# RMSNorms in blocks of 344 tokens inside the phase that uses them, in a float32 hybrid decoder step

## The reference

```python
def rmsnorm(x, g):
    return x * lax.rsqrt(jnp.mean(x * x, axis=-1, keepdims=True) + EPS) * g
def swiglu(h, w_in, w_out):
    gu = h @ w_in
    return (jax.nn.silu(gu[..., :2816]) * gu[..., 2816:]) @ w_out
for i in range(2):
    hn = rmsnorm(x, norm_mix_g[i])
    x = x + (gated_deltanet(hn, ...) if i == 0 else s5_mixer(hn, ...))
    x = x + swiglu(rmsnorm(x, norm_ffn_g[i]), w_ffn_in[i], w_ffn_out[i])
y = rmsnorm(x, final_norm_g)
```

## Time and profile before

| | us |
|---|---|
| median of 3 executions | 3890.07 |
| the profiled execution | 3887.29 |
| its span, first to last instruction | 3885.5 |
| PE busy / DVE / ACT / POOL | 3545.1 / 2123.1 / 845.5 / 836.9 |
| mean granted TensorE clock | 0.959 |

### The profile page before, as it was taken

One profiled execution on the slowest core, in us unless ns is written; L12 is line 12 of the kernel. 1 busy time (PEld: TensorE's weight loads), 2 busy tenths in 40 slices (PEclk: granted clock), 3 DMA queues, 4 the chain that ended last, 5 costly groups with the idle time before them and its releaser, 6 DMA issues.

```text
span 3885.5 us, 56613 instructions
## 1 busy us (share of the span) xinstructions
PE 3545.1 (91%) x23849; PEld 3439.2 (89%) x23849; DVE 2123.1 (55%) x4331; ACT 845.5 (22%) x1691; POOL 836.9 (22%) x773
## 2 busy tenths in 40 slices
PE   4999999999999999997889999997679699999997
PEld 3989999998989898996879999996569699999997
DVE  3576757566666767575477577554632333333424
ACT  2333232423333332323100110111210210000001
POOL 1202020201111020201223232322323133323331
PEclk7999999999999999999989999999779899999998
DMA  2101010101001010100112222223831011111111
GB/s 78 34 23 36 28 41 17 41 23 40 29 30 40 23 36 28 35 17 29 33 40 75 71 70 77 71 77 110 231 90 49 22 44 49 44 50 49 45 49 55
DMA packets 91965, 197.29 MB, mean 51 GB/s; under 512 B 23232, under 2 KB 51008, under 8 KB 90560
## 3 DMA queue, kind: packets, MB, share of 16 engines
q1 hardware_dynamic: 65344, 152.42, 12.1%
q10 hardware_dynamic: 26368, 41.25, 3.2%
HBM read 152.69 MB, written 40.94 MB: 50 GB/s over the span
## 4 chain that ended last, share of the span: by engine, by line
PE 78%; DVE 17%; issue 2%; ACT 2%; DMA 1%; SPq 1%; POOL 0%; ACTq 0%; DVEq 0%; POOLq 0%
PE ps L210 25%; PE ps L464 14%; PE ps L1162 11%; PE ps L634 4%; PE ps L548 4%; PE ps L630 4%; PE ps L620 3%; PE ps L240 2%; PE ps L488 1%; DVE dwork L1095 1%; PE ps L523 1%; PE ps L536 1%; DVE hlo L269 1%; DVE S L987 1%; PE ps L476 1%
## 5 line engine op out<-in xcount | busy, mean ns | idle before, releaser
L210 PE MATMUL ps<-hhi,whi 128*128 128x344 f32 x2520 | 811.5, 322 | 87.2 <-DVE hlo L269 72.2
L210 PE MATMUL ps<-hhi,wlo 128*128 128x344 f32 x2520 | 808.8, 321 | 0.0
L210 PE MATMUL ps<-hlo,whi 128*128 128x344 f32 x2520 | 807.9, 321 | 0.0
L1843 POOL TENSOR_TENSOR wtick<-wtick 128x1 f32<-128x1 f32 x213 | 43.0, 202 | 2846.8 <-PE ps L210 977.6
L210 PEld LDWEIGHTS ps<-hhi,whi 128*128 128x128 f32 x2520 | 477.4, 189 | 90.5 <-issue 66.2
L1846 POOL TENSOR_TENSOR wlo<-wraw,whi 128x1024 fp32r<-128x1024 f32 x213 | 527.5, 2477 | 17.1
L210 PEld LDWEIGHTS ps<-hhi,wlo 128*128 128x128 f32 x2520 | 476.8, 189 | 0.0
L210 PEld LDWEIGHTS ps<-hlo,whi 128*128 128x128 f32 x2520 | 476.5, 189 | 0.0
L1215 DVE TENSOR_TENSOR ab<-ps,sg 128x344 f32<-128x344 f32 x132 | 68.2, 516 | 639.5 <-PE ps L210 628.1
L464 PE MATMUL ps<-hhi,whi 128*128 128x344 f32 x1152 | 386.2, 335 | 4.4 <-DVE dwork L847 1.9
L1162 PE MATMUL ps<-ahi,whi 128*128 128x344 f32 x1056 | 342.7, 325 | 32.3 <-DVE ab L1215 29.9
(11 more groups left out here) (328 smaller groups left out, 6092.2 us busy)
## 6 DMA issues: line engine op xcount, KB each, us to landing
wraw<-in_w SPq DMA_DIRECT2D x213, 512.0 KB, 3.3
tab<-keep_tab SPq DMA_DIRECT2D x8, 1088.0 KB, 6.4
S<-in_sin ACTq DMA_DIRECT2D x16, 512.0 KB, 3.5
out_sout<-S ACTq DMA_DIRECT2D x16, 512.0 KB, 2.6
keep_u<-hs SPq DMA_DIRECT2D x8, 580.0 KB, 3.0
uu<-keep_u SPq DMA_DIRECT2D x8, 580.0 KB, 7.9
keep_tab<-cp ACTq DMA_DIRECT2D x8, 576.0 KB, 6.1
keep_y<-yg SPq DMA_DIRECT2D x64, 68.5 KB, 2.3
```

The source lines that it names most:

```text
L210: ins = nc.tensor.matmul(out, w, r[:, kt, blk(n)], start=k == 0, stop=k == 3 * KT - 1)
```

## The change

**By blocks.** The prolog's, the two FFN norms and the last one go by blocks of 344 tokens. Squares and `nh` now lie in a ring of six places of 344 columns in the same memory (`RING`). DVE makes part of the squares: in block 0 the odd tiles, in block 1 tiles 0 to 3; in the last norm the odd tiles of block 2. `nh`, `hhi` and `hlo` of block 0 can be made when block 0's sums are there.

**In one phase.** n1, n3 and fin are no phases any more. ffn0 and ffn1 begin with the norm: PE makes the sums of blocks 0 and 1, then, when block 0 is ready, the gate and the up unit of f = 0, j = 0 for block 0 alone (`project_pair`); then the sums of block 2, the pair for block 1, the pair for block 2. In the prolog PE makes all 24 sums and then projects block by block. ffn1's last output units go block by block too (`piece`), with the last norm's sums of a block behind the next block's pieces.

**Issue.** The operations are issued by `go`, with waits for single steps. x is loaded in three transfers, one a block, and y stored in four (block 0, block 1, two halves of block 2). The ACT table is loaded ahead of the wait for x in the prolog, and right behind the last `ahi` copy in ffn1.

```diff
+        def project_pair(p, units, banks, names, ready):
+            at = [wait_weights(p, u) for u in units]
+            for n in range(NC3):
+                ready(n)
+                for u, s, bank, name in zip(units, at, banks, names):
+                    out = ps[:, bank(n), 0:NB]
...
+                    p.go(ins, f"{name}{n}")
+                    plan[("PE", f"unit{u}")] = p.n
+        RING = 6
+        def square_by(n, kt, last=False):
+            if last:
+                return "DVE" if n == 2 and kt % 2 else "ACT"
+            return "DVE" if (n == 0 and kt % 2) or (n == 1 and kt < 4) else "ACT"
+        def sums(p, n, bank, last=False):
+            w = "f" if last else ""
+            b = bank("ACT", w + f"ln{n}")
+            for kt in range(KT):
+                p.after(square_by(n, kt, last), w + f"sq{n}.{kt}")
+                p.go(nc.tensor.matmul(ps[:, b, 0:NB], ones[:, :], ring(nsq, KT * n + kt), ...), w + f"ss{n}.{kt}")
+        def square(e, n, kt, ready=None, last=False):
+            k = KT * n + kt
+            if k >= RING:
+                e.after("PE", w + f"ss{(k - RING) // KT}.{(k - RING) % KT}")
...
+        def norm_blocks_act(a, ready=None):
+            nc.scalar.preload_act_table_set(LOGEXP)
+            mine = [(n, kt) for n in range(NC3) for kt in range(KT) if square_by(n, kt) == "ACT"]
+            ahead = [s for s in mine if KT * s[0] + s[1] < KT + RING]
+            rest = mine[len(ahead):]
+            for n, kt in ahead:
+                square(a, n, kt, ready)
+            for n in range(NC3):
+                root(a, n)
+                for kt in range(KT):
+                    a.after("DVE", f"h{n}.{kt}")
+                    a.go(nc.scalar.activation(hhi[:, kt, blk(n)], ring(nh, KT * n + kt), AF.Copy), f"hi{n}.{kt}")
+                    if rest and (n == 0 or kt < 2):
+                        square(a, *rest.pop(0), ready)
+        def norm_blocks_dve(v, gi, ready=None):
...
+            for k in range(NC3 * KT + 2):
+                n, kt = divmod(k, KT)
+                if n < NC3:
+                    if k >= RING:
+                        v.after("DVE", f"lo{(k - RING) // KT}.{(k - RING) % KT}")
+                    v.after("ACT", f"rms{n}")
+                    v.go(V.scalar_tensor_tensor(ring(nh, k), x[:, kt, blk(n)], gains[:, gi, kt:kt + 1], nr[:, blk(n)], ALU.mult, ALU.mult), f"h{n}.{kt}")
+                if k >= 2:
+                    n, kt = divmod(k - 2, KT)
+                    v.after("ACT", f"hi{n}.{kt}")
+                    v.go(V.tensor_tensor(hlo[:, kt, blk(n)], ring(nh, k - 2), hhi[:, kt, blk(n)].bitcast(F32), ALU.subtract), f"lo{n}.{kt}")
...
         def ffn_pe(ph):
+                sums(p, 0, take)
+                sums(p, 1, take)
+                def block_ready(n):
+                    if n == 1:
+                        sums(p, 2, take)
+                    normed(p, n)
...
+                        if ph == "ffn1" and f == NF:
+                            for n in range(NC3):
+                                for m in range(KT):
+                                    piece(m, n)
+                                if n:
+                                    sums(p, n - 1, take, True)
+                            sums(p, NC3 - 1, take, True)
...
         def ffn_act(ph):
+                norm_blocks_act(a)
...
+                if ph == "ffn1":
+                    nc.scalar.preload_act_table_set(LOGEXP)
+                    for n, kt in mine[:KT + RING]:
+                        square(a, n, kt, added, True)
+                    root(a, 0, True)
+                    for n, kt in mine[KT + RING:]:
+                        square(a, n, kt, added, True)
+                    root(a, 1, True)
+                    store_y(a, 0, 0, KT)
+                    root(a, 2, True)
+                    store_y(a, 1, 0, KT)
+                    store_y(a, 2, 0, KT // 2)
+                    store_y(a, 2, KT // 2, KT)
...
         def ffn_dve(ph):
+                norm_blocks_dve(v, 1 if ph == "ffn0" else 3)
...
+                    for kt in range(1, KT, 2):
+                        square(v, NC3 - 1, kt, added, True)
+                    for n in range(NC3):
+                        v.after("ACT", f"frms{n}")
+                        for kt in range(KT):
+                            v.go(V.scalar_tensor_tensor(x[:, kt, blk(n)], ...), f"y{n}.{kt}")
...
-            sp.dma_start(x[:, :, :], dr["x"]).then_inc(in_x, 16)
+            for n in range(NC3):
+                sp.dma_start(x[:, :, blk(n)], dr["x"][:, :, blk(n)]).then_inc(in_x[n], 16)
```

More of the change, by code:

```diff
@@ L79, in build @@
         const_ready = sem("const_ready")
-        in_x = sem("in_x")
+        in_x = [sem(f"in_x{n}") for n in range(NC3)]
         in_par = sem("in_par")
@@ new lines, in square @@
+        def square(e, n, kt, ready=None, last=False):
+            w = "f" if last else ""
+            k = KT * n + kt
+            if k >= RING:
+                e.after("PE", w + f"ss{(k - RING) // KT}.{(k - RING) % KT}")
+            if ready is not None:
+                ready(n, kt)
+            if e.who == "ACT":
+                e.go(nc.scalar.activation(ring(nsq, k), x[:, kt, blk(n)], AF.Square), w + f"sq{n}.{kt}")
+            else:
+                e.go(nc.vector.tensor_tensor(ring(nsq, k), x[:, kt, blk(n)], x[:, kt, blk(n)], ALU.mult), w + f"sq{n}.{kt}")
@@ L271, in build, with normed @@
+        def normed(p, n):
+            p.after("DVE", f"lo{n}.{KT - 1}")
         eps_t = sb("eps_t", [P, 4])
@@ L1166, in ffn_pe, with piece @@
-            return body
+                        def piece(m, n):
+                            s = wait_weights(p, unit(ph, e, 4 + m // 4))
+                            out = ps[:, take("DVE", f"x{e}.{m}.{n}"), 0:NB]
+                            q = 0
+                            for kt in range(2):
+                                c = kt * 512 + m % 4 * P
+                                for w, r in ((whi, ahi), (whi, alo), (wlo, ahi)):
+                                    ins = nc.tensor.matmul(out, w[:, s, c:c + P], r[:, e % 2, kt, blk(n)], start=q == 0, stop=q == 5)
+                                    q += 1
+                            p.go(ins, f"out{e}.{m}.{n}")
+                            if n == NC3 - 1:
+                                plan[("PE", f"unit{unit(ph, e, 4 + m // 4)}")] = p.n
```

118 lines of the change are left out of this document (57 added, 61 removed).

## The result

The changed kernel took 3840.6 us (median of four runs, 3840.5 to 3841.4) where the kernel before took 3888.8; the ratio is 0.9879, 95% interval 0.9862 to 0.9896. Forecast were 3831 and the range 3818 to 3849. The unaltered changed kernel, run again in a later session, took 3845.5, ratio 0.9901 (0.9885 to 0.9918). So 38 to 48 us are saved of the 56.5 that the prediction added up (before took 3883.1 beside the later runs).

What follows compares the result with a forecast made beforehand. Four serial stages holding 165 us were taken as what the change touches: prolog 23.0, FFN norms 12.2 and 10.4, tail 10.9 saved, 56.5 in sum. From 3887.3 that gives 3830.8, stated as 3831; own range 3824 to 3840, whole range 3818 to 3849.

Steps and rivals of the forecast that it cites:

- the four serial stages: Prolog, two FFN norms and tail: three engines work in turn, none full; they hold 165 us, gains forecast at 56.5.
- hidden by that: FFN norms, POOL's 3.6 us split for the next weight slot: covered by the slot being freed 3.8 earlier, so no cost.
- Rival A: Small operations don't overlap on their engine once each has its own wait: 3847 us; chance 0.16.
- stall: FFN norms: ACT, and DVE with it, stands 11.7 us at block 2's square until that block's first sum frees a ring place.
- the price of the second clock fall: First FFN norm, PE's gap of 4.4 us: if the clock falls there too, 2.7 us, ending at 55.3 instead of 52.7.
- the charge of 0.7 for the squares beside a split: First FFN norm: POOL splits until 1819.2 and may slow DVE's new squares; 0.7 us off the gain, bounds 0 to 2.3.
- Rival B: The clock holds in the gaps of 4.4 us and nothing collides on the port: 3822 us; chance 0.14.
- Rival D: The clock stays low in the four stages as PE works in bursts: slower than before, 3923 us; chance 0.02.
- I charge 2 of 6.8: Prolog: POOL's splits of weight units 0 and 1 beside h and lo cost 2 us of 6.8, bounds 0 and 6.8.
- Rival C: Prolog: x in short rows lands slowly, so the prolog's whole gain is gone: 3855 us; chance 0.05.
- a start after 11: Prolog: the first sum, forecast at 10.6 us; starting after 11 was named as a sign that the prediction is wrong.
- The last store then takes what it takes now: Tail: from the last product y to the end of the span 3.1 us, as in the kernel before.

## Why the prediction was right, and where it was off

*The bound.* Right: the four serial stages held the time and gave 52.8 of the 56.5 us forecast. Not all that moved outside them is scatter: 1.9 us in FFN 0 and 0.5 in FFN 1 came with the new norms. 0.5 of each is a term that the prediction put at nothing, the split "hidden by that" behind the pair: PE waited 0.2 for it, and the unit took 11.80 for 11.32.

*Prices of small operations.* Right: product and subtraction came at 0.92 a tile, the y products at 0.49. Rival A (no overlap) is out.

*First and second FFN norm.* The order of events was right, and most times to 0.3: stall 11.80 for 11.7, pauses 7.0 and 4.2 for 7.3 and 4.4, block 0 ready at 18.6 for 18.4, block 1 at 37.7 for 37.5. Off was the price of the second clock fall: 2.7 taken for each, and with the clock held the run shows 2.5 for the first and 1.55 for the second. Too high too was the charge of 0.7 for the squares beside a split: they did collide (one square took 2.67 for 0.50), but the first root was done 8.3 after the table load for 8.1. So the ends came at 54.7 for 55.3, and 55.9 or 57.5 for 58.2. Rival B had the clock hold in the short pause; the windows show it at 0.50. Rival D had it stay low; over the two norms it is 0.88 and 0.84, for 0.70 and 0.66. The rule that the prediction cited (the Trainium skill, TensorE: Matmul & The Clock Gate, section Loop structure matters more than you think) holds here for pauses of 4.2 us too. Before's own trace could have told: in FFN 0 PE waits 4.04 at 1960.87, and the clock is at 0.50 behind it.

*Prolog.* The step that failed is "I charge 2 of 6.8": it was 5.9, nearly the upper bound. The forecast without any charge was 49; 49 and 5.8 are the 54.8 that came. The prediction had the cue beside it, a subtraction of 2.72, and the rule that a VectorE operation with two SBUF inputs excludes GpSimd's (the Trainium skill, SBUF — State Buffer, section Who interferes with whom); the rule was right and the discount had no row behind it. Rival C is out: block 0 of x landed at 10.7, little after the 9.5 to 10.3 forecast. But the first sum began at 11.4, and the prediction had named a start after 11 as a sign that it is wrong. It did no harm: the first product came at 19.7 for the 20 forecast.

*Tail.* The failed term is "The last store then takes what it takes now", 3.1. It took 6.3. I carried over a duration from a kernel whose stores kept pace with the products (by its 398 GB/s an estimated 1.33 us of transfer for 516 KB, one every 1.33) to one that lets block 0's store wait until 3825.0 and issues 2752 KB from 3828.9 on. The rest was right: the products end 45.6 after the output pieces begin, for 45.4.

*The sum.* 3.8 too much in the prolog, 3.4 in the tail, 3.5 too little in the norms, and 6.0 in a stretch that was not touched, of which 1.9 came with the new norms. So the total was 10 above the forecast, inside the range but just above the likeliest case's own (3824 to 3840), and 14 above in the later session. That it was no further off is partly luck: the norms gave 3.5 more than forecast, the first by prices set too high, and so hid most of the prolog's 3.8.

## What to carry to other kernels

When a stage is cut into blocks and its engines overlap, follow each in-order queue: here a ring of six buffers with its release behind 48 matmuls cost 8 us of a norm, and moving eight instructions up gave it back. Two engines that never met before will meet when one moves earlier; charge the whole collision, or move the other one's work too. A store's time behind the last product went here by the bytes outstanding (6.3 us twice with 2752 KB just issued, 3.15 with stores of 516 KB that kept pace), not by a constant. And before a difference of 5 us is explained, profile the unaltered kernel a second time.
